# The order of an intermediate gate tensor in DRAM: by token chunk, or by group of four keys

## What is computed

```python
def block(xb):                                            # 128 tokens at a time
    q = (xb @ w_query).reshape(tb, PEER_HEADS, 2, PEER_HALF)
    s = jnp.einsum('thpc,hpnc->thpn', q, sub_keys)
    top_s, top_i = lax.top_k(s, PEER_TOPK)                # 16 of 128, for each half key
    ...                                                   # 16 best of the 256 sums, softmax: g
    h = gelu(einsum('thkd,td->thk', expert_u[idx], xb))
    return einsum('thk,thkd->td', g * h, expert_v[idx])
```

## Time and profile before

| | us |
|---|---|
| median of 3 runs | 2973.97 (2970.5 to 2981.79) |
| the profiled execution | 2976.31 |
| its span, first to last instruction | 2974.5 |
| PE busy | 2643.6 (89%) |
| DVE busy | 2434.8 (82%) |
| POOL busy | 1254.2 (42%) |
| ACT busy | 871.1 (29%) |
| DMA moved | 685.26 MB, mean 230 GB/s |

### The profile page before, as it was taken

The page is one execution under the profiler, slowest core; times in us unless marked ns, Lnnn a source line. Parts: engine busy times, 40 slices in busy tenths (PEclk is TensorE's granted clock), DMA queues, the critical chain, the costliest instruction groups (busy, mean ns, idle before and its releaser), DMA issues.

```text
span 2974.5 us, 47235 instructions
## 1 busy us (share of the span) xinstructions
PE 2643.6 (89%) x17293; PEld 1732.6 (58%) x17459; DVE 2434.8 (82%) x4517; ACT 871.1 (29%) x1463; POOL 1254.2 (42%) x833
## 2 busy tenths in 40 slices
PE   8999888698867674589999999999999999999996
PEld 3566655458867663445555555555555555555553
DVE  3244545574999999589999999999999999999998
ACT  2333333211114444522222222222222222222223
POOL 2110000210000000066666666676667677776772
PEclk9999979799988985689999999999999999999998
DMA  4000010261002223699999999999999999999994
GB/s 153 22 15 15 15 71 15 93 244 48 1 1 114 113 103 160 251 374 351 361 350 353 342 357 344 338 356 347 335 345 337 348 331 350 342 337 338 335 333 177
DMA packets 262960, 685.26 MB, mean 230 GB/s; under 512 B 35624, under 2 KB 118184, under 8 KB 258352
## 3 DMA queue, kind: packets, MB, share of 16 engines
q0 software_dynamic: 110592, 402.70, 36.2%
q1 hardware_dynamic: 152240, 280.98, 26.9%
HBM read 624.89 MB, written 58.72 MB: 230 GB/s over the span
## 4 chain that ended last, share of the span: by engine, by line
PE 20%; issue 13%; DVE 11%; DMA 10%; POOL 2%; SPq 1%; DVEq 0%; ACT 0%; POOLq 0%
PE o_psum L1879 10%; PE h_psum L1861 10%; DMA early<-v_blocks,pick_index 6%; DMA fetched<-v_blocks,pick_index 3%; DVE wide L1731 3%; DVE early L1727 2%; DVE early L1702 2%; DVE v_split L1713 1%; POOL early L1670 1%; DVE wide L1719 1%; DMA fetched<-u_rows,pick_index 1%; DVE act_out L1690 1%; DVE w_split L1694 1%; SPq L2009 1%; POOL fetched L1670 1%
## 5 line engine op out<-in xcount | busy, mean ns | idle before, releaser
L1861 PE MATMUL h_psum<-early 128*128 128x384 bf16 (+1 forms) x6144 | 863.2, 301 | 25.5 <-issue 14.9
L1879 PE MATMUL o_psum<-v_split,w_split 128*128 128x512 bf16 x3713 | 826.9, 380 | 24.6 <-DVE wide L1719 13.4
L1861 PEld LDWEIGHTS h_psum<-early 128*128 128x128 bf16 x6144 | 604.0, 98 | 284.2 <-issue 31.7
L1879 PEld LDWEIGHTS o_psum<-v_split,w_split 128*128 128x128 bf16 x3840 | 375.4, 98 | 456.3 <-DVE wide L1719 18.5
L1670 POOL DMA_INDIRECT early<-v_blocks,pick_index x320 | 488.7, 1527 | 225.4 <-DVE wide L1731 137.4
L1670 POOL DMA_INDIRECT early<-u_rows,pick_index x320 | 448.3, 1401 | 320.1 <-DVE dots L1727 201.5
L1731 DVE SCALAR_TENSOR_TENSOR wide<-early,dots,wide 128x1024 f32<-128x1024 f32 x320 | 402.2, 1282 | 37.3 <-DMA early<-v_blocks,pick_index 33.6
L1727 DVE CUSTOM_DVE_ANT_0 early<-early,wide 128x1024 f32<-128x1024 f32 x320 | 382.1, 1217 | 36.5 <-DMA early<-u_rows,pick_index 31.5
L1617 ACT ACTIVATE w_split<-act_out 128x640 bf16<-128x640 f32 x128 | 94.3, 737 | 633.5 <-DVE act_out L1690 582.2
L1604 ACT ACTIVATE act_out<-h_psum 128x384 f32<-128x384 f32 (+1 forms) x256 | 97.6, 433 | 597.1 <-PE h_psum L1861 546.9
L1101 PE MATMUL r_t_psum<-rt_x_t,early 128*128 128x128 f32 (+1 forms) x1920 | 236.7, 285 | 0.0
(11 more groups left out here) (201 smaller groups left out, 2976.3 us busy)
## 6 DMA issues: line engine op xcount, KB each, us to landing
early<-u_blocks SPq DMA_DIRECT2D x128, 512.0 KB
early<-v_blocks SPq DMA_DIRECT2D x128, 512.0 KB
gates<-wide SPq DMA_DIRECT2D x20, 2048.0 KB, 6.4
gate<-gates SPq DMA_DIRECT2D x32, 1280.0 KB
early<-w_query SPq DMA_DIRECT2D x8, 1024.0 KB, 5.8
att_w_raw<-w_fox SPq DMA_DIRECT2D x4, 1536.0 KB, 6.8
early<-u_rows,pick_index POOLq DMA_INDIRECT x320
early<-v_blocks,pick_index POOLq DMA_INDIRECT x320
```

Source lines behind the costliest of these rows:

```text
L1861: mm = pe.matmul(h_psum[k][:, half, 0:width * P], u_split[:, k, part, c], xs[:, first:first + width, xpart, c, :], start=(c == 0 and part ...
L1879: mm = pe.matmul(o_psum[(DENSE * p + t) % 2][:, half * 512:half * 512 + 512], w_split[:, p, q, part, t * P:(t + 1) * P], v_split[:, p, q, ...
```

## The change

The tensor `gates` in DRAM gets another order of its axes. Before, it is [partition, chunk of tokens, key, token in the chunk]; after, it is [partition, group of 4 keys, chunk of tokens, key in the group and token in the chunk]. Its size, the buffers in SBUF, the number of DMAs, their order, and all waits stay as they are. In a store, a partition's 16 KB now go to 32 places of 512 bytes, 10 KB apart; in a load, a partition's 10 KB are one run.

```diff
 def store_gates(i):
     for k in range(2):
         sp.wait_ge(g_copied, (2 * i + k + 1) * (CHUNK // 4) + 2)
-        sp.dma_start(gates[:, bass.ds(2 * i + k, 1)].rearrange("p o h t -> p (o h t)"),
-                     stage[:, k].rearrange("p h t -> p (h t)")).then_inc(stage_stored[k], 16)
+        sp.dma_start(gates[:, :, bass.ds(2 * i + k, 1)].rearrange("p g o n -> p (g o) n"),
+                     stage[:, k].rearrange("p (g h) t -> p g (h t)", h=GROUP)
+                     ).then_inc(stage_stored[k], 16)
...
 def load_gate(g, p):
-    sp.dma_start(gate[:, p], gates[:, :, bass.ds(g * GROUP, GROUP), :]).then_inc(gate_in[p], 16)
+    sp.dma_start(gate[:, p].rearrange("p c h t -> p (c h t)"),
+                 gates[:, bass.ds(g, 1)].rearrange("p o c n -> p (o c n)")).then_inc(gate_in[p], 16)
...
-gates = nc.dram_tensor("gates", (P, TOKENS // CHUNK, N_KEYS, CHUNK), F32, kind="Internal").ap()
+gates = nc.dram_tensor("gates", (P, N_KEYS // GROUP, TOKENS // CHUNK, GROUP * CHUNK), F32, kind="Internal").ap()
```

## The result

| | before | after |
|---|---|---|
| median of 6 runs each, us | 2978.36 (2970.5 to 2984.21) | 3001.7 (2997.54 to 3006.8) |
| span of the profiled execution | 2974.5 | 3005.0 |
| PE, DVE busy | 2643.6, 2434.8 | 2664.7, 2432.7 |

A forecast was written before the change was run, and what follows sets the result against it. PE was taken to bound the experts' first half, DVE delayed by DMA the second, DMA the start. Stores +2.2, start -4.5, second half -10 give 12.3 us less: 2961.7 us from the median, range 2951 to 2979.

The forecast's parts named there:

- What the packets do: Gate loads and stores: short packets move from loads to stores, so packets under 2 KB stay near 118000.
- What a short packet costs: Gate loads: 4.4 us each with 512-byte packets, 3.2 with long ones, 1.2 us less a load (0.9 to 1.8).
- The stores: Routing: a store lands after 8.6 us, not 6.4, without ACT waiting; the last one costs +2.2 us (0 to 4.8).
- The start: Start of the expert phase: DMA-bound, gate loads delay other data; 4.5 us shorter (1 to 8).
- the term for DVE's first gate multiplication: Start of the expert phase: DVE's long wait for the first `wide` tiles ends 3.6 us earlier.
- The second half of the experts: 2329 to 2912 us: shorter gate loads take 1.2 us off DVE's 2.4 us waits a load; 10 us gained (0 to 12.2).
- The first half: First 1026 us of the expert phase: PE has no gaps, so the saving there costs and brings 0.
- slower, by the length of packets: Expert phase: rows wait behind 10 KB packets; costly above 2.4 us a load, at 3.5 +13 us, 2987; chance 0.07.
- The rival "nothing": Whole kernel: packet length doesn't matter, or only start and stores move; 2971.7 to 2974; chance 0.22.

The follow-up runs named there:

- Run 5: Changed kernel with 256 bytes of gap in DRAM after each 512 bytes of the table, so loads read 512-byte runs: 2975.2 us, ratio 0.9972.
- run 2: Changed kernel with a gap in the SBUF gate buffer after every fifth chunk, making 2560-byte runs: 2991.3 us, ratio 1.0033.
- run 9: Kernel before, table and stores untouched, each gate load reading one 10 KB run per partition (not the group's gates): 2999.0 us, ratio 1.0056.
- run 7: Kernel before with each gate load cut in four DMAs of 5 chunks, one issued after each of four blocks: 2958.6 us, ratio 0.9916.
- run 8: Changed kernel with each gate load cut in four DMAs of 5 chunks, one issued after each of four blocks: 2963.4 us, ratio 0.9940.
- run 11: Changed kernel with gaps in DRAM (reads of 512 bytes) and each gate load spread over four blocks: 2958.9 us, ratio 0.9923.

## Why the prediction was wrong

**What the packets do: right.** 118184 packets under 2 KB stayed 118184.

**What a short packet costs: right.** The rates were to be over 380 GB/s behind a gate load, and they are 418 against 364. A packet of 512 bytes took 29 ns and one of 10 KB 393, so the 160 short packets of an engine's share of a load come to 4.6 us, and the 8 long ones to 3.1; 4.4 and 3.2 were expected. On runs of 512 bytes the engines do lose throughput.

**The stores: right.** 8.6 us to landing were expected and 9.1 measured, +2.2 for the last and +2.4 measured, no wait of ACT. Run 5, whose stores are the same, is faster than the kernel before.

**The start: right in the sum, less so in its parts.** 4.5 us were expected and it is 4.7 shorter. But the term for DVE's first gate multiplication, 3.6 us, measured 2.4 (20.7 us after the phase begins in place of 23.1), and the rest came after it, where 1.2 had been allowed.

**The second half of the experts: wrong, and this is the step that failed.** It says that while a gate load is in the engines "a row comes up to that much later", so that a load of 3.2 us in place of 4.4 takes 1.2 us off DVE's 2.4. That treats the load as a block of engine time that the rows stand behind, shorter when it is faster. In place of -1.2 us a load the waits near a load grew from 2.2 to 3.6. The sizes of 4.4 and 3.2 us were right, but the load was never a block: before, its 4.6 us of engine time lay spread over 13 us, after, its 3.1 over 4. The load and the rows share the engines, and what counts for DVE is how much of them the rows get in the first ten microseconds. With short runs the gate load is slow and lets the rows by; with long ones it takes what it needs at once. DVE does not need the gates for another whole group. It needs the rows in a few microseconds, since the ring holds 6 tiles. The change made fast what had time, at the cost of what had none. Runs 2, 5 and 9 show that the run length does this; runs 7, 8 and 11 show that the same bytes cost PE nothing once they don't come together.

**The first half: wrong.** "The same saving there costs and brings 0; what hides it is PE itself." It hid a gain, but I had not asked how much of a loss it could hide. DVE had 60 us of gaps in 1026 there, 3.0 a group, of which over 2 were already waits for rows. So only some 0.7 us a group was free. From the first down product to the end of that half DVE's waits for rows grew from 45.0 to 76.1 us, 1.5 a group; that ran through the cover, and each of 19 groups became 1.06 us longer, as much as in the second half. Some 0.8 of this follows from the waits alone; the clock and the uneven spread of the waits are likely for the rest, which isn't shown. This is also why the rival "slower, by the length of packets" was too small: it has the mechanism and the point of decision, 3.5 us a load, but counted 15 us of loss, for 14 groups; over all 30 it is 32 in the traces. And it had no term for PE's clock, which fell at four of PE's longer waits and cost 8.5 us.

**Where the chances went wrong.** That rival was given 0.07. Against it I put that the short runs "evidently didn't let rows pass, or DVE would not wait 1.54 us behind them". A wait of 1.5 us shows that short runs delay the rows; it says nothing on whether longer ones would delay them more. The trace of before held no load of long runs beside rows, which was named as open, and it should have carried more of the chance. The rival "nothing" is refuted, and with it, for this kernel, the figure of 512 B for line rate of the Trainium skill's page "DMA: Bandwidth & Descriptors", section Specifications: 512-byte loads were slower by the rates of the trace, and the kernel with them faster.

**What is shown of the sharing, and what is argued.** From 4 to 7 us after the issue, when both kinds of transfer are in the engines, the number of a gate load's packets to each 4 KB packet of a row is 1.0 with 10 KB, 1.2 with 5 KB, 1.4 with 2560 bytes and 4.4 with 512. So from 2560 bytes up an engine gives nearly one run of the load for one of a row, and the rows' share falls as the load's runs get longer; of the short runs it takes some four. With 2560 bytes the rows have in these 3 us nearly what they have with 512 (219 and 232 GB/s), and less from 8 to 10 us (256 and 302). The Trainium skill's page "DMA: Bandwidth & Descriptors", section "Queues, rings and completion order", says that an engine takes turns between queues packet by packet, a packet being several descriptors. The traces don't say which engine a packet went through, so they show no single turn; with 512 bytes they agree with several runs a turn, with the longer ones a turn looks like one run. That four DMAs do as one fits this.

That 5120 bytes wait as long in all as 2560 (92.8 and 97.1 us) has two sides in the packets: the rows move less from 4 to 7 us, 162 GB/s against 219, but 95% of the load has started by 8.7 us and not by 10.7. That the two cancel is an argument, not a measurement. Why run 5 beats the kernel before by 0.28% stays open.

## What to carry to other kernels

A transfer that two consumers' data share the engines with has two numbers, its length and its due time. Making the one that is due late faster, by longer runs, can delay the one that is due soon, so before widening the runs of a bulk load look in the waits at who stands behind it, and how much slack that engine has. The better remedy here was not the layout but the time of issue: the load cut in quarters and issued one after each block took 22 us off the kernel before, with its short runs and its layout unchanged.

## What the runs showed of the hardware

A load on 16 partitions can occupy all 16 DMA engines at a fraction of their rate: the same 1.25 MB in eight DMAs of 16 neighbouring partitions held the engines busy at 187 GB/s for 12 us, where one DMA on 128 partitions moved 418, and the kernel took 240 us longer than before. With every eighth partition it was 151 us. A packet of 10 KB took 877 ns with neighbours, 695 with every eighth partition and 393 in one DMA. Part of the time is PE's clock, which stood at 0.50 for some 171 and 99 us after 1305 us; at half speed that costs 85 and 50 us. By the formula in the Trainium skill's page "SBUF — State Buffer", section "Door 1: The DMA port swizzle", these two reach 4 and 8 of 16 ports. The order of the rates, 236 and 285 GB/s against 418, agrees with it; the factor of 2 between the two doesn't show.

The two sides of a DMA need not be cut alike: with gaps of 32 bytes in SBUF only, after each 512 bytes, the trace has two packets of 5 KB for a run of 10 KB. Such a packet took 249 ns, against 203 with 5 KB pieces in SBUF, and this was the worst form of a single load, 3028 us, some 26 us over the changed kernel.

PE's granted clock fell to 0.50 in four of nine places where PE stood for 2 to 4 us between two down products, and came back after 3.4 to 6.8 us. Short waits of the busiest engine can so cost more than their own length: with four of them, 10.6 us of standing, came 17 us at half speed.
